# A ring of twenty weight pieces in place of sixteen in the expert stage of a two-block model

## What is computed

```python
logits = h @ w_router + b_router              # 512 x 32
top_val, top_idx = lax.top_k(logits, 4)       # four experts for each token
gates = softmax(top_val)
# the 2048 (token, expert) pairs are sorted by expert and cut into blocks of rows of one expert
gu  = rows @ w1[e] + b1[e]                    # w1[e]: 1024 x 2048
act = clamped_swiglu(gu)                      # 1024 wide
y   = act @ w2[e] + b2[e]                     # w2[e]: 1024 x 1024
```

## Time and profile before

| what | us |
| --- | --- |
| three runs | 3733.55, 3733.76, 3737.01 |
| median | 3733.76 |
| the profiled execution, whole | 3736.16 |
| its span, first to last instruction | 3734.0 |
| expert stage in it (first bias matmul of block 0 to the end of block 47) | 979.95 to 2180.6 |

### The profile page before, as it was taken

One profiled execution on the slowest core, in us unless ns is written; L12 is line 12 of the kernel. 1 busy time (PEld: TensorE's weight loads), 2 busy tenths in 40 slices (PEclk: granted clock), 3 DMA queues, 4 the chain that ended last, 5 costly groups with the idle time before them and its releaser, 6 DMA issues. The chain is left out here.

```text
span 3734.0 us, 63179 instructions
## 1 busy us (share of the span) xinstructions
PE 3306.2 (89%) x25517; PEld 2106.7 (56%) x25518; DVE 1399.2 (37%) x2384; ACT 984.8 (26%) x1766; POOL 154.9 (4%) x221
## 2 busy tenths in 40 slices
PE   3998788787799987999999987997889989878998
PEld 2877677686333322333333336875578778655787
DVE  5535545545211110111111136544643365446333
ACT  2323313312111111111111103333532133435321
POOL 0000000001200000000000010000000000000000
PEclk8999889887799999999999988997999999979999
DMA  6621220224769899997986963321023143310231
GB/s 216 239 94 31 98 96 6 98 71 181 298 250 396 316 400 400 401 372 289 397 301 247 384 264 116 97 48 45 1 90 91 46 122 98 52 35 1 91 102 57
DMA packets 273123, 647.38 MB, mean 173 GB/s; under 512 B 36890, under 2 KB 97050, under 8 KB 270978
## 3 DMA queue, kind: packets, MB, share of 16 engines
q1 hardware_dynamic: 251314, 605.12, 45.5%
q0 software_dynamic: 6224, 21.24, 1.8%
q10 hardware_dynamic: 15360, 17.82, 1.5%
HBM read 600.85 MB, written 43.27 MB: 173 GB/s over the span
## 5 line engine op out<-in xcount | busy, mean ns | idle before, releaser
L1697 PE MATMUL ps<-raw,ex_xT 128*64 128x512 f32 x3072 | 704.8, 603 | 31.4 <-DMA raw<-in_w_dram 30.9
L1697 PEld LDWEIGHTS ps<-raw,ex_xT 128*64 128x64 f32 x3072 | 206.4, 137 | 436.4 <-issue 367.3
L1788 DVE TENSOR_SCALAR ex_gl<-ps 128x256 f32<-128x256 f32 x96 | 40.8, 425 | 1040.7 <-PE ps L1697 1040.7
L1697 PE MATMUL ps<-raw,ex_aT 128*64 128x512 f32 x1536 | 353.3, 597 | 13.9 <-DMA raw<-in_w_dram 13.2
L1697 PEld LDWEIGHTS ps<-raw,ex_aT 128*64 128x64 f32 x1536 | 104.2, 136 | 217.5 <-issue 185.0
L1949 PE MATMUL ps<-zhi,hl 128*128 128x512 f32 (+1 forms) x448 | 169.7, 379 | 0.0
L1947 PE MATMUL ps<-zhi,hh 128*128 128x512 f32 (+1 forms) x448 | 169.1, 377 | 0.6 <-DVE hl L2077 0.6
L1948 PE MATMUL ps<-zlo,hh 128*128 128x512 f32 (+1 forms) x448 | 168.5, 376 | 0.0
L2494 PE MATMUL ps<-uu_hi,hh 128*128 128x512 f32 x384 | 151.6, 395 | 12.2 <-DVE uu_lo L2606 12.2
L2496 PE MATMUL ps<-uu_hi,hl 128*128 128x512 f32 x384 | 152.8, 398 | 0.0
L2495 PE MATMUL ps<-uu_lo,hh 128*128 128x512 f32 x384 | 152.3, 397 | 0.0
(11 more groups left out here) (558 smaller groups left out, 6018.9 us busy)
## 6 DMA issues: line engine op xcount, KB each, us to landing
raw<-in_w_dram SPq DMA_DIRECT2D x384, 1024.0 KB, 18.5
oT<-in_w_in_dram SPq DMA_DIRECT2D x64, 512.0 KB, 3.6
u_raw<-in_w_in_dram SPq DMA_DIRECT2D x24, 1024.0 KB, 5.1
expert_out<-xn SPq DMA_DIRECT2D x4, 4096.0 KB, 16.7
expert_out<-ex_yrow ACTq DMA_DIRECT2D x98, 128.0 KB, 6.2
late_ada<-in_w_ada_dram SPq DMA_DIRECT2D x12, 1024.0 KB
early_w<-in_w_in_dram SPq DMA_DIRECT2D x10, 1024.0 KB, 6.6
mT<-in_w_ada_dram SPq DMA_DIRECT2D x4, 2048.0 KB, 19.9
```

The costliest lines, as they stand in the source:

```text
L1697: mm = pe.matmul(o, x, M["raw"][:, slot, k, h * 512:(h + 1) * 512], start=(s >= 8 and kk == 0), stop=(kk == 7))
```

## The change

`RING` becomes 20. `RING_AT` moves down by 4 x 8192 bytes, to where the router stage keeps its scratch (`rt_...` tensors and others). To leave the first sixteen pieces at the addresses that they had, piece n is put into the place (n mod 20 + `LATE_SLOTS`) mod 20, with `LATE_SLOTS` = 4. So the slots 16 to 19 are the ones at the low addresses, and they are first filled after the router stage, like slots 9 to 15.

```diff
-RING = 16
+RING = 20
+LATE_SLOTS = 4
 EARLY = 9
 RING_AT = 229344 - RING * 8192
...
             for g in range(EARLY):
-                sp.dma_start(M["raw"][:, g, :, :], piece_source(A, g // 12, g % 12)).then_inc(raw_in[g], 16)
+                sp.dma_start(M["raw"][:, (g + LATE_SLOTS) % RING, :, :], piece_source(A, g // 12, g % 12)).then_inc(raw_in[g], 16)
...
                     sp.wait_ge(used, w * NP + s + 1)
-                    sp.dma_start(M["raw"][:, slot, :, :], piece_source(A, e + ahead // NP, ahead % NP)).then_inc(raw_in[slot], 16)
+                    sp.dma_start(M["raw"][:, (slot + LATE_SLOTS) % RING, :, :], piece_source(A, e + ahead // NP, ahead % NP)).then_inc(raw_in[slot], 16)
 
             sp.wait_ge(gathered, 16)
             for g in range(EARLY, NS):
-                sp.dma_start(M["raw"][:, g, :, :], piece_source(A, g // NP, g % NP)).then_inc(raw_in[g], 16)
+                sp.dma_start(M["raw"][:, (g + LATE_SLOTS) % RING, :, :], piece_source(A, g // NP, g % NP)).then_inc(raw_in[g], 16)
...
-                                mm = pe.matmul(o, x, M["raw"][:, slot, k, h * 512:(h + 1) * 512], start=(s >= 8 and kk == 0), stop=(kk == 7))
+                                mm = pe.matmul(o, x, M["raw"][:, (slot + LATE_SLOTS) % RING, k, h * 512:(h + 1) * 512], start=(s >= 8 and kk == 0), stop=(kk == 7))
...
             with pe.Fori(0, E // EU) as i:
                 for j in range(EU):
                     expert(i, j)
+            for j in range(E % EU):
+                expert(E // EU, j)
...
-        at = RING_AT + EARLY * 8192
+        at = RING_AT + (LATE_SLOTS + EARLY) * 8192
```

## The result

| | before | after |
| --- | --- | --- |
| median of four runs, us | 3733.66 (3729.51 to 3737.01) | 3699.54 (3695.41 to 3708.11) |
| ratio, with its 95% interval | | 0.9912 [0.9891, 0.9933] |
| the profiled execution, whole | 3736.16 | 3708.11 |
| its span | 3734.0 | 3706.0 |
| expert stage in it | 1200.7 | 1172.25 |

The change makes the kernel 0.9% faster. The direction and the places are those of the forecast.

What follows compares the result with a forecast made beforehand. TensorE was taken as busy but starved by DMA in runs of single-block experts; four slots would gain 10.24 + 10.24 + 3.05 + 2.2 = 25.7 us, so 3733.76 - 25.7 = 3708.0 us, range 3702 to 3720.

Steps and rivals of the forecast that it cites:

- C: Block 33 of the expert stage, costing 3.05 us beyond 23.6 us a block; all of it was to be gained.
- D: Block 47 of the expert stage, costing 2.2 us beyond 23.6 us a block; all of it was to be gained.
- The wait for the ring: TensorE's expert-stage matmuls waiting for DMA of a weight piece: to fall from 44.2 us to near 28.
- What was costed at nothing: Eleven early loads at stage start, unmoved addresses, SyncE's loop of five reloads, TensorE's loop of five experts: no cost forecast.
- A: Blocks 8 and 9 of the expert stage, costing 11.7 us beyond 23.6 us a block; 10.24 us to be gained.
- rival 1: TensorE's code is fetched at each loop turn, one wait of 2 to 4 us: about 3720 us; chance 0.09.
- Rival 2: Code fetches at TensorE's loop turns queue behind weights, up to 15.6 us a turn: 3770 us, slower; chance 0.04.
- Rivals 3: Rival 3: loads in flight, not slots and bandwidth, limit short experts, so four slots give nothing: 3733.8 us; chance 0.05.
- rival 4: Half a gain: lead after A not rebuilt in time, or later stages move a few us: 3708 to 3720; chance 0.05.
- B: Blocks 14 to 19 of the expert stage, costing 49.1 us beyond 23.6 us a block; 10.24 us to be gained.
- the other price, 2.72: A starved block's 32.7 us over 12 pieces, including gather and writes; would make the whole gain 27.1 us; not taken.
- the lower edge of the range: Whole kernel time: 3702 us, from 27.1 us of gain and 3.5 us between earlier runs (3703), and a little.

Runs made afterwards that it cites:

- e2: The kernel before the change (sixteen slots) run again without an edit: 3732.45 us, ratio 0.9993 to the kernel before.
- e6: The kernel before (sixteen slots) with TensorE's last four experts placed behind its loop: 3735.42 us, ratio 1.0000.
- e1: The changed kernel (twenty slots) run a second time without an edit: 3704.19 us, ratio 0.9908 to the kernel before.
- e7: The changed kernel (twenty slots) run a third time without an edit: 3705.21 us, ratio 0.9921 to the kernel before.
- e9: The changed kernel with twenty-one slots, seven experts in TensorE's loop, six tensors moved to x's place: 3705.43 us, ratio 0.9926 to the kernel before.
- e10: The changed kernel with nineteen slots, nineteen experts in TensorE's loop, which never turns: 3722.62 us in a single run.
- e4: The changed kernel, still twenty slots, with ten experts in TensorE's loop instead of five: 3712.01 us, ratio 0.9938 to the kernel before.
- e5: The changed kernel with twenty-two slots, eleven experts in TensorE's loop, six tensors moved to x's place: 3703.88 us, ratio 0.9914 to the kernel before.

## Why the prediction was right, and where it was not

**The mechanism held.** Four slots let the stream run ahead in the long experts, and give that lead back in the runs of short ones. The stream itself is unchanged (2.56 us a piece, 32.1 to 32.7 us a starved block). C and D are gone, 3.05 and 2.15 us, as forecast (0.1 us of D is left). The wait for the ring is 27.2 us, where "near 28" was forecast.

**What was costed at nothing, cost nothing.** The stretch before A (blocks 1 to 7) is 165.24 us long, 165.23 before, with eleven loads in a row ahead of it. The addresses and the longer SyncE loop show nowhere. Outside the stage the spans of before, e2 and e6 have 2533.4, 2530.5 and 2528.4 us, those of after, e1 and e7 2533.7, 2533.4 and 2527.7. In e9 and e10, whose profiled executions are long for their stage, they are 2540.8 and 2540.7: this part scatters by more than the misses that are asked about here.

**Rivals 1 and 2, code at the turns: out for this change, true for a larger one.** No packet came at a turn with 72 kB, and the unedited kernel has no block over 23.6 us at 21, 28 or 37. With some 145 kB the very thing of rival 1 is there: a wait at the upper end of its 2 to 4 us, and 1.5 to 1.7 us more in the block behind it, about 5.5 us a turn. Rival 2 needed 6.4 us a turn for a loss and forecast 15.6; even the large loop shows no such price. That queue 8 carries TensorE's code is shown by e6; the sizes of 72 and 145 kB stay estimates from the 65 bytes per recorded instruction. Counted in experts, loops of four, five and seven turn without a packet at the turn (before, after, e9), and loops of ten and of eleven with packets there (e4, e5). At one packet of 16.4 kB an expert, as in e6, the first three are 66, 82 and 115 kB and the other two 164 and 180.

**Rivals 3 and 4, no lead or half a gain: out.** The series from seventeen to twenty-two slots shows the lead in A, B, C and D each; after A it is built again in full, since B gained no less than A. That code in another place would cost a few us, the other half of rival 4, fell with e6.

**The step that failed: the gain of 10.24 us at A and at B.** Over the pairs of traces A gave 10.5 to 11.0 us (first pair: 58.94 - 48.12 = 10.8) and B 11.6 to 12.9 (first pair 190.71 - 178.36 = 12.35; e2 against e1, the smallest, 11.6). The price of 2.56 us for a piece is not what failed: the starved pieces are as far apart as before, and the traffic beside the weights is the same in both kernels, as the working said. So the other price, 2.72, has no ground, though its 10.9 is about what A gave; that is a coincidence. What the term left out is the restart. It took all four pieces as worth their period and the stream as otherwise unchanged, but with twenty slots the stream begins again with a piece of w2 in place of one of w1, and that first load lands about 1 us sooner (5.1 and 5.2 us against 5.9 and 6.5), and 0.4 MB more have moved 24 us later. With 1.0 us at each of the two places the terms are 11.2 and 11.2 and the sum is 27.7; measured are 10.8 at A and 12.2 at B on the mean, and 27.3 to 28.6 for the stage. That the earlier landing passes on to the whole stretch is worked out, not shown by a run of its own. Some 1 us at B stays open: from one profile to another a stretch moves by 1 to 2 us, and the mean value of a slot in B over the whole series is 2.3 us, not 3.

**The second miss: the lower edge of the range.** It came from 27.1 us and from 3.5 us by which three runs of one kernel differed. Three runs show little of a spread: the seventy of that kernel reach over 20 us, the fourteen of the changed one over nearly 17. Taken together, the 4.8 us between 3708.0 and 3703.2, the median of all fourteen, are 2.2 for the stage (27.9 on the mean of the pairs, less 25.7) and some 2.6 that no stretch shows; the other 3.7 down to 3699.5 are the chance of the first four runs.

**What stays open.** The means of all runs differ by 30.7 us, the stages in the traces by 27.9. The standard error of the first is 1.4 and the stage of the kernel before itself lies between 1199.6 and 1205.1 in three traces, so that the 1 to 3 us left may be chance; no run shows that they are. Nor is it known why the steps from eighteen to twenty slots are larger than those around them; the restart accounts for about 1 us of the last.

**A better version.** None is shown. With twenty-two slots the stage is 2.8 us shorter than with twenty, but the whole time is 3703.9 against 3703.2, and with twenty-one it is 3705.4.

## What to carry to other kernels

The deeper ring did not make the stream faster here: the starved pieces are 2.56 us apart with sixteen slots and with twenty. Its worth can be estimated as the number of new slots times the period of a starved piece, once at every place where TensorE starves after the DMA engines have stood idle, and never more than that place costs now. Traffic that comes once a work unit does not enter, since it is the same before and after (2.10 MB of gathers in both kernels from the restart to the end of B); but look with which piece the stream begins again, for that is estimated to have moved each place here by about 1 us. Cut the stage where the work units begin and write down the excess of each; the sum of the smaller of lead and excess is the gain, and the places run out one by one as slots are added.

Before unrolling further to fit a ring's period, look at what the engine's instruction queue fetches at a turn: here none came at the turns of loops of four, five and seven experts, and those of ten experts, where packets came, cost some 5.5 us each. And where a forecast is to be good to 0.1%, let the range come from the spread of many runs, not from three.

## What the runs showed of the hardware that was not expected

- TensorE's loop body was kept with seven experts (some 101 kB by the 65 bytes; one packet on queue 8 in 800 us) and not with ten (some 145 kB), where 26 packets come and a turn costs 3.9 to 4.0 us of waiting, and 1.5 to 1.7 us more in the block that follows. Code that is passed once was fetched without a gap (e10: 8 packets in 307 us, TensorE busy throughout).
- The first 1 MiB load after 3 us or more without weight traffic landed after 5.9 to 6.7 us when it was a piece of w1 (sixteen to nineteen slots) and after 4.8 to 5.6 us when it was one of w2 (twenty to twenty-two, one exception at 6.5; at the start of the stage piece 9, of w2, landed after 4.8 to 5.1 with sixteen, seventeen and nineteen to twenty-two).
- Executions of one kernel spread with a standard deviation of 4 to 5 us in 3700, with nothing that differs in the program. The granted clock over the whole span goes along with it loosely: of the changed kernel, 3708.11 and 3707.8 at 0.934, and 3695.41, 3696.52 and 3697.33 at 0.939; but 3712.19 at 0.935 and 3701.85 at 0.940, so it does not order the runs.
- The same program with eighteen slots cost 8.6 us in A in one execution and 6.3 in the next, while its stretches without gaps agree to 0.02 us: here a stretch in which the DMA engines are the limit (share 1.03) was less repeatable than one in which TensorE is.
